# A decoder block on one Trainium2 core: fewer attention parts weighted ahead of the first mix, and a steeper start of the interleaved retrieval

## The reference, cut to what matters

```python
h = rms_norm(x, g[0]) * (1 + scale1) + shift1
q, k, v, glu, gates = split(h @ w_in)
outs, lses = dilated attentions of three groups (4 heads each)
attn = sum(softmax(lses, over groups) * outs) @ w_attn_o
conv = silu(layer_norm(depthwise_conv(a * sigmoid(b)))) @ w_conv_o
y = (sigmoid(g_attn) * attn + sigmoid(g_conv) * conv) @ w_out
x = x + gate1 * rms_norm(y, g[1])
h = rms_norm(x, g[2]) * (1 + scale2) + shift2
# retrieval: per token 8 heads x 16 experts out of 16384
expert, gate = top-k of the product keys of h @ w_q
pre = einsum('td,tkd->tk', h, expert_down[expert])
y = einsum('tk,tkd->td', gelu(pre) * gate, expert_up[expert])
x = x + gate2 * rms_norm(y, g[3])
```

## Time and profile before

| | us |
|---|---|
| median of 3 runs (lowest, highest) | 4179.17 (4174.87, 4181.80) |
| the profiled execution, its own time | 4181.56 |
| its span | 4178.9 |
| PE busy | 2812.1 |
| DVE busy | 2278.5 |
| POOL busy | 1387.0 |
| ACT busy | 541.3 |

### The profile page before, as it was taken

How to read it: one execution, slowest core, us unless ns; L and a number is a source line. 1 busy time by engine, 2 the same in 40 slices (tenths; PEclk the granted TensorE clock), 3 DMA queues, 4 the chain that set the end, 5 groups by cost and what they waited for, 6 DMA issues and landing times.

```text
span 4178.9 us, 37663 instructions
## 1 busy us (share of the span) xinstructions
PE 2812.1 (67%) x15140; PEld 1595.7 (38%) x15140; DVE 2278.5 (55%) x3525; ACT 541.3 (13%) x1191; POOL 1387.0 (33%) x1109
## 2 busy tenths in 40 slices
PE   5999899899899999997973434434444444434435
PEld 3787788798755554553540100101101100101101
DVE  6399779642643333325664565664656664444442
ACT  3211221201200101012120100100100110000000
POOL 2321211010022333322334454534434444344342
PEclk9999999999899999998985555555555555555556
DMA  9353332898467898986879999999999999999998
GB/s 365 141 231 111 152 137 105 310 414 314 182 234 307 354 380 337 357 331 241 339 288 421 388 406 421 421 422 421 421 421 418 421 422 419 418 422 421 421 421 371
DMA packets 201837, 1413.23 MB, mean 338 GB/s; under 512 B 24384, under 2 KB 24512, under 8 KB 31936
## 3 DMA queue, kind: packets, MB, share of 16 engines
q0 software_dynamic: 152064, 1107.36, 64.6%
q1 hardware_dynamic: 43680, 291.53, 18.4%
q10 hardware_dynamic: 5920, 11.94, 0.8%
HBM read 1403.35 MB, written 7.39 MB: 338 GB/s over the span
## 4 chain that ended last, share of the span: by engine, by line
PE 41%; DMA 39%; DVE 11%; POOL 4%; issue 3%; ACT 2%; ACTq 0%; DVEq 0%; SPq 0%; POOLq 0%
PE psum L605 41%; DMA front<-in_down,back 30%; DMA front<-in_up,back 6%; DVE front L1604 4%; POOL front L576 3%; DVE back L1372 2%; DVE back L1341 1%; DMA front<-in_w_conv_o 1%; ACT back L1134 1%; POOL x_low L560 1%; DMA back<-in_x 1%; DVE back L1705 0%; ACT front L1238 0%; DVE back L1595 0%; DMA back<-in_up,back 0%
## 5 line engine op out<-in xcount | busy, mean ns | idle before, releaser
L605 PE MATMUL psum<-front 128*32 128x512 f32 (+2 forms) x6608 | 1393.9, 661 | 914.2 <-DMA front<-in_up,back 854.0
L1604 DVE CUSTOM_DVE_ANT_0 front<-front,back 128x2048 f32<-128x2048 f32 x512 | 1170.8, 2292 | 1372.7 <-DMA front<-in_down,back 1240.6
L605 PEld LDWEIGHTS psum<-front 128*32 128x32 f32 (+1 forms) x6608 | 566.7, 160 | 1676.4 <-issue 1422.9
L576 POOL DMA_INDIRECT front<-in_down,back x512 | 595.7, 1163 | 909.2 <-DVE back L1604 671.5
L605 PE MATMUL psum<-back,front 128*32 128x128 f32 (+3 forms) x4400 | 645.1, 462 | 333.3 <-DMA back<-in_up,back 173.0
L576 POOL DMA_INDIRECT front<-in_up,back x442 | 511.2, 1157 | 1020.3 <-PE psum L605 968.5
L605 PEld LDWEIGHTS psum<-back,front 128*32 128x32 f32 (+1 forms) x4400 | 376.5, 169 | 608.7 <-issue 343.5
L554 POOL TENSOR_TENSOR w_low<-front,w_high 128x2048 fp32r<-128x2048 f32 x33 | 155.2, 4702 | 539.1 <-ACT w_high L1022 539.1
L605 PE MATMUL psum<-x_high,w_high 128*128 128x512 f32 x640 | 252.3, 394 | 9.4 <-POOL x_low L560 6.6
L605 PE MATMUL psum<-x_low,w_high 128*128 128x512 f32 x640 | 251.0, 392 | 0.0
L605 PE MATMUL psum<-x_high,w_low 128*128 128x512 f32 x640 | 250.7, 392 | 0.0
(11 more groups left out here) (161 smaller groups left out, 1677.0 us busy)
## 6 DMA issues: line engine op xcount, KB each, us to landing
front<-in_w_in SPq DMA_DIRECT2D x116, 1024.0 KB, 7.0
back<-in_ada_w SPq DMA_DIRECT2D x64, 1024.0 KB, 7.8
front<-in_ada_rows POOLq DMA_DIRECT2D x32, 1024.0 KB, 13.6
front<-in_w_out SPq DMA_DIRECT2D x32, 1024.0 KB, 5.8
front<-in_w_q SPq DMA_DIRECT2D x32, 1024.0 KB, 5.1
front<-in_w_conv_o SPq DMA_DIRECT2D x16, 1024.0 KB, 8.6
front<-in_w_attn_o SPq DMA_DIRECT2D x16, 512.0 KB, 11.3
front<-in_down,back POOLq DMA_INDIRECT x512, 20.4
```

The source lines that it names most:

```text
L576: nc.gpsimd.indirect_dma_start(out=row_, out_offset=None, in_=table[:, :], in_offset=bass.IndirectOffsetOnAxis(ap=idx4[:, t % 2, c:c + 1], ...
L605: return nc.tensor.matmul(o, a, b, start=start, stop=stop)
L1604: V.tensor_tensor_reduce(d_row[s], d_row[s], h2r, 1.0, 0.0, ALU.mult, ALU.add, pre[:, b // 16 % 2, b % 16:b % 16 + 1]).then_inc(dots_done, 1)
```

## The change

Two things. In `tail(0)` the weighting of the attentions becomes a function `combine(t)`. Only tile 0 is weighted ahead of the first mix; tiles 1 to 3 are weighted between the first "ao" mix and the first "co" mix. Of the first column group's eight pieces of the `ada_rows` sum, two instead of five stand ahead of the "ao" mix, none instead of one between the mixes, and six instead of two behind them. In `tail(1)` PACE begins 3, 6, 9, 12, 15, 18, 21, 24 and goes on in even steps from 24 to 128: the ninth number is 25 where it was 13, the eleventh 28 where it was 16, and the last is 128 in both.

```diff
--- before.py
+++ after.py
@@ -120,7 +120,9 @@
 
 def block_pace():
 
-    return [(i + 1) * 128 // tail_chunks(1) for i in range(tail_chunks(1))]
+
+    rest = tail_chunks(1) - 8
+    return [3 * (i + 1) for i in range(8)] + [LAG + (i + 1) * (128 - LAG) // rest for i in range(rest)]
 
 
 PACE = block_pace()
@@ -1478,7 +1480,9 @@
             st.link(V.reciprocal(ln_r, ln_std))
             for c in range(CO):
                 V.tensor_tensor(cv[:, c, :], cv[:, c, :], ln_r, ALU.mult).then_inc(ln_norm, 1)
-            for t in range(TT):
+
+            def combine(t):
+
                 dve.wait_ge(og_in[t], 16)
                 for g in range(NG):
                     for h in range(HG):
@@ -1491,6 +1495,8 @@
                             dve.wait_ge(og_used, HG * (NG * t + g - 1) + h + 1)
                             ins = V.scalar_tensor_tensor(dst, part, cf, dst, ALU.mult, ALU.add)
                         ins.then_inc(og_used, 1)
+
+            combine(0)
 
             def modulation(j):
 
@@ -1662,7 +1668,7 @@
                 wide = [P, 4, n]
                 for cg in range(4):
                     if c == 0:
-                        condition(2 + cg // 2, 8 * (cg % 2), 8 * (cg % 2) + 5)
+                        condition(2 + cg // 2, 8 * (cg % 2), 8 * (cg % 2) + (5 if cg else 2))
                     passed(c, 9)
                     for m in range(4):
                         dve.wait_ge(act_took, ATOOK[c, "ga", cg] + m + 1)
@@ -1670,7 +1676,10 @@
                         mixed = mixT[:, mix_at(4 * cg + m), tok]
                         V.tensor_tensor(mixed, mixed, ps[:, m, 0:n], ALU.mult).then_inc(dve_took, 1)
                     passed(c, 2)
-                    if c == 0:
+                    if c == 0 and cg == 0:
+                        for t in range(1, TT):
+                            combine(t)
+                    if c == 0 and cg:
                         condition(2 + cg // 2, 8 * (cg % 2) + 5, 8 * (cg % 2) + 6)
                     for m in range(4):
                         dve.wait_ge(act_took, ATOOK[c, "gc", cg] + m + 1)
@@ -1682,7 +1691,7 @@
                         V.tensor_tensor(mixed, mixed, sgc[:, m, 0:n], ALU.add).then_inc(mix_ready, 1)
                     passed(c, 1)
                     if c == 0:
-                        condition(2 + cg // 2, 8 * (cg % 2) + 6, 8 * (cg % 2) + 8)
+                        condition(2 + cg // 2, 8 * (cg % 2) + 6 if cg else 2, 8 * (cg % 2) + 8)
                         if cg == 0:
                             modulation(0)
                             modulation(1)
```

## The result

| | us |
|---|---|
| before, median of 4 runs (lowest, highest) | 4179.35 (4174.87, 4181.80) |
| changed, median of 4 runs (lowest, highest) | 4217.22 (4214.92, 4220.10) |
| ratio, 95% interval | 1.0087 (1.0075 to 1.0100) |
| span of the profiled execution, changed | 4217.3 |

A forecast was written before the change was run, and what follows sets the result against it. It took PE to bound `tail(1)`, the DMA the second half and the gate and branch chunks of `tail(0)`. Terms -4 + 48 - 2 - 4 gave +38 on 4179.2, so 4217 us, range 4198 to 4234.

The forecast's parts named there:

- Part one: First mix of `tail(0)`: PE's 13.63 us wait for DVE goes, but the full DMA leaves only -4 us.
- sign (1): `tail(0)`: no PE wait before the first "co", more waits for weight chunks before 963, last "co" at 957 to 961.
- The mix: First "ao" mix of `tail(1)`: twelve more dot products ahead of it on DVE, +48 us, mix near 1287.
- sign (3): `tail(1)`: PE idle 25 to 30 us ahead of "ao" and some 25 more around it, "co" near 1283.
- What comes back: `tail(1)`: two `weighted_rows` blocks done inside the wait, -2 us, and gaps closing in the rest, -4 us.
- The DMA-bound rest: After `tail(1)`, fetching blocks 128 to 511: as long as before, 1993 us.
- (a): Gathers in `tail(1)` run at the bus's rate, 2.5 us a dot product, no loss: 4167 to 4177 us; chance 0.11.
- (b): `tail(0)` keeps its whole 13.6 us gain and the lighter rest closes gaps: +21, 4200 us; chance 0.14.
- (c): `tail(1)`: chains over ACT and `weighted_rows` end last, nothing comes back: +56, 4235 us; chance 0.12.
- (d): The `tail(1)` stall is not on the path, time within a few us: 4179 us; chance 0.02.

The follow-up runs named there:

- e5_early_exp_changed: The changed kernel with ACT's exponent for token tile 0's last gates moved ahead of the first "ga" sigmoids of `tail(1)`; 4194.66 us, ratio 1.0031.
- e1_part_one_only: The changed kernel with the PACE table of before, so only the `tail(0)` weighting and `ada_rows` pieces are moved; 4172.88 us, ratio 0.9994.
- e7_light_rows_before: The kernel before, with 28 of the 32 `ada_rows` pieces loading only a quarter of their columns; 4165.16 us, ratio 0.9958.
- e8_light_rows_part_one: The changed kernel's `tail(0)` with the PACE table of before, 28 of 32 `ada_rows` pieces loading only a quarter of their columns; 4153.51 us, ratio 0.9929.
- e2_pace_only: The kernel before with the new PACE table only; 4216.54 us, ratio 1.0089.
- e3_ninth_19: The changed kernel with PACE's ninth number 19 instead of 25, then even steps to the same numbers from chunk 60 on; 4193.58 us, ratio 1.0039.
- e6_early_exp_part_one: The changed kernel with the PACE table of before and ACT's exponent moved ahead of the first "ga" sigmoids of `tail(1)`; 4169.20 us, ratio 0.9974.
- e4_ninth_10: The changed kernel with PACE's ninth number 10 instead of 25, then even steps to the same numbers from chunk 60 on; 4172.89 us, ratio 0.9989.

## Why the prediction was right, and where its terms were not

The total is right to a microsecond, and that is luck: the largest term was 9 us too large, and three smaller ones, one of them scatter, made up for it. The mechanism, a mix of `tail(1)` held up by twelve more dot products, is what the runs show.

The sum was -4 + 48 - 2 - 4 = +38. The profile gives, for the same four stretches and a fifth:

| term | forecast | measured | from |
|---|---|---|---|
| what part one leaves at the start of the dot products | -4 | -2.2 | 1184.60, 1182.39 |
| the later "ao" mix of `tail(1)`, start of "co" | +48 | +38.8 | 36.6 + 2.2 |
| blocks done in the wait, and gaps that close | -6 | -2.4 | 34.2 - 36.6 |
| the DMA-bound rest | 0 | +4.2 | 38.4 - 34.2 |

**Part one: right in mechanism.** The wait went as described, and the bounds from the share (2.0 us) and from the bytes (6.2 us) enclose the 4.0 us of the 1.7 MB and the 4 to 6 us that the profiles show from the first "ao" to `w_out`. The -2.2 of the table is smaller, but it is one pair, and 1.4 of it come from the length of the first chunk of `tail(1)`, which takes 10.56 to 13.61 us in the twelve profiles with either `tail(0)`. The lighter loads show that the full DMA was the reason. The prediction expected waits for chunks in its place; for column group 1 it named a wait for DVE only as a possibility, and that is where 9.84 of them stand. The waits for chunks came to 7.6 us before `w_out`, in the kernel before to 8.6, so that part of sign (1) failed; the last "co", at about 960, came as it says.

**The mix: right in mechanism, over-sized by 9 us.** The step that erred is the pace, "mostly 3.7 to 4.0 without weights and 4.9 for the last three", counted from number 13 on. The 13th dot product, which I left where it was, ends 49.2 us after the start of number 0 instead of 54.1, and the last twelve come every 3.63 us, near the 3.5 of the lower end. I had counted ACT's moved Gelu as covered and did not ask what it does to the DMA: PE stops at 1218.4, not at 1230.9, and uses no chunks from there. Whether that helps the gathers is not shown. It can explain only what came after 1218, and 2.2 of the 4.9 us were there before it (dot product 9 starts 35.1 us after number 0, in the kernel before 37.4). And the first twelve dot products of `e5_early_exp_changed` came every 3.59 us with PE busy throughout. The first twelve take 3.59 to 4.31 us each in the twelve profiles, and the kernel before, from which I took my 4.31, is the slowest of them.

The wait of PE between the two "ao" chunks was over-sized too, 14.1 us where sign (3) has some 25. I let the gather `expert_up` 0 be issued at 1263 and land at 1276; it was issued at 1257.61, and the row of PE that waits for it starts 7.9 us later. It changed nothing in the sum, since that chain ran beside the dot products.

**What comes back: not decided.** It was -2.4 us in this pair. PE's gap at block 32 closed (3.9 us at the longest, 0.7 now), but waits of 2.26 us for a gather and of 2.84 and 3.35 us for DVE stand in the same stretch. "The pace of the gathers against PE is tied" was the right reason to expect little. But the stretch from "co" to the end of `tail(1)` scatters by more than this term: it took 931.8 us in the kernel before and 929.3, 930.2 and 937.2 in `e1_part_one_only`, `e7_light_rows_before` and `e8_light_rows_part_one`, with the same table; with the steep table 929.4, 921.9 and 930.5 in the changed kernel, `e2_pace_only` and `e5_early_exp_changed`. In `e2_pace_only` PE was busy 865.5 us of it, in the changed kernel 871.6. The -6 of the forecast is within that.

**The DMA-bound rest: the same length, and +4.2 us of scatter.** In all twelve profiles from the same point to the end it took 2007.8 to 2012.0 us; the kernel before has the shortest and the changed kernel the longest of them, and the ten others lie between, with either table (2009.4 in `e1_part_one_only` and in `e2_pace_only`). It made the total look better than its terms. With 2010 us in both, the difference would be 34 us in this pair of executions, against 38 by the medians.

**The rivals.** (a), gathers at the bus's rate, needed 2.5 us a dot product: no profile has the first twelve, or the twelve behind them, faster than 3.59. With three buffers in turn the period of a buffer was 3 x 3.63 = 10.9 us, of which the dot product is 2.3. The rule of the Trainium skill (DMA: Bandwidth & Descriptors, Anatomy of one DMA) gives an estimate of 4.4 us for a gather of 1 MB. The trace does not agree: the shortest of all gathers of the kernel before took 5.4 us to land, and those at this place 8.0 to 11.8. (b), the whole of part one kept, is refuted by `e1_part_one_only`. (c), the chain over ACT and `weighted_rows`, ended 0.15 us before the dot products, and `e3_ninth_19` shows that without it the mix is late all the same. (d), the stall not on the path, falls with `e2_pace_only`, `e3_ninth_19` and `e5_early_exp_changed`: "co" starts 44.0, 17.9 and 11.4 us later than in the kernel before, and their spans are 35.7, 16.4 and 13.1 us longer, which is the same within the scatter named above.

## What to carry to other kernels

Work that is interleaved by a table costs what it takes at the place where the table makes a busy engine wait for it, not on average: here twelve more dot products ahead of one small multiplication cost PE 38 us, and doing them early saved nothing measurable later in a stage that PE bounds. Before steepening such a table, find what releases the first of the steps; moving one exponent of 0.2 us gave a head start of 26 us that no number in the table could give. And before removing a stall, look at the DMA share around it: here, at 0.94 to 1.01, about 8 of 13.6 us were only moved.

## What the runs showed of the hardware that I had not expected

POOL's issue of a gather is not of one length. In the changed kernel it took 0.93 us or 1.9 to 3 us, as in these rows of its timeline:

```profile
1209.61 0.93 POOL L578 DMA_INDIRECT front<-in_down,back  x1 [5.46 <-DVE back L1610]
...
1220.09 3.00 POOL L578 DMA_INDIRECT front<-in_down,back  x1 [3.85 <-DVE back L1610]
```

The long one began inside a dot product (1219.98 to 1222.27), the short one 0.35 us before one (1209.96). The others between 1184 and 1290 follow the same pattern: those that began while a dot product ran are the long ones, and each of them ends 0.8 us after that dot product, as here (1220.09 + 3.00 = 1223.09). So an issue that begins inside a dot product is held until the dot product ends.

With three buffers in turn that delay is a part of the period. Of the nine gathers for dot products 3 to 11, six had a long issue in the kernel before (4.31 us a dot product), four in the changed kernel (3.91), three in `e6_early_exp_part_one` (3.82) and two in `e5_early_exp_changed` (3.59). It is not the only cause: `e2_pace_only` has six at 3.93, `e4_ninth_10` four at 4.28. I have not tried it by itself, so what it costs in all stays open.
